# The sample tile inside the last prompt group of the delta rule, its state updates inside the output projection, and three handovers of a hybrid decoder step rearranged

## The reference

```python
def gated_delta_rule(q, k, v, g, beta, s0):          # 4 heads, keys and values 128 wide
    ...                                              # per chunk: kb, lower triangle, triangular solve -> u, w
    def step(state, inp):
        qd, kd, uc, wc, att, cd = inp
        v_new = uc - wc @ state
        out = qd @ state + att @ v_new
        state = state * cd + kd.T @ v_new
        return state, out
    s_fin, outs = lax.scan(step, s0, xs)

o, s_fin = gated_delta_rule(dq, dk, dv, g, beta, s0)   # s0 = 0 for the prompt, a given state for each sample
o = rms_norm(o, delta_norm_w) * silu(bz)
h = x + concatenate([a_out, o]) @ w_out                # output projection, 1024 x 1024
hn = rms_norm(h, norm_ffn_w)
qh = hn @ w_pq                                         # queries, 1024 x 2048
sub = einsum(qh, sub_keys)                             # scores on 2 x 128 keys, top 16 of each half, top 16 of the pairs
y = h + sum(gate * gelu(u_e . hn) * v_e)               # over the chosen experts of 16384
```

## Time and profile before

| | us |
|---|---|
| median of 3 runs | 2228.98 (2225.56 to 2231.54) |
| profiled execution | 2227.2 |
| its span, first to last instruction | 2225.4 |
| PE busy | 2014.9 (91%) |
| DVE busy | 1540.5 (69%) |
| POOL busy | 1158.6 (52%) |
| ACT busy | 771.4 (35%) |

### The profile page before, as it was taken

How to read it: one execution, slowest core, us unless ns; L and a number is a source line. 1 busy time by engine, 2 the same in 40 slices (tenths; PEclk the granted TensorE clock), 3 DMA queues, 4 the chain that set the end, 5 groups by cost and what they waited for, 6 DMA issues and landing times.

```text
span 2225.4 us, 34386 instructions
## 1 busy us (share of the span) xinstructions
PE 2014.9 (91%) x12706; PEld 1898.6 (85%) x12706; DVE 1540.5 (69%) x2782; ACT 771.4 (35%) x1228; POOL 1158.6 (52%) x632
## 2 busy tenths in 40 slices
PE   5999899787768997999898999999899999999998
PEld 5989855576658896988888998999799999999998
DVE  2377555434251105689985999964489999999996
ACT  3224144323212323444344444433323333333332
POOL 2235100123032232567576444458788888888884
PEclk9999799998759898999999999999999999999999
DMA  5664365343422354577678687789888989899894
GB/s 185 221 239 163 137 191 175 110 184 150 161 98 85 131 233 158 167 238 231 212 241 264 239 304 253 303 323 384 303 311 318 311 310 328 308 317 313 308 324 135
DMA packets 176595, 520.94 MB, mean 234 GB/s; under 512 B 15152, under 2 KB 86064, under 8 KB 170704
## 3 DMA queue, kind: packets, MB, share of 16 engines
q1 hardware_dynamic: 136560, 290.94, 37.5%
q0 software_dynamic: 36864, 134.23, 17.9%
q10 hardware_dynamic: 3056, 94.24, 10.8%
HBM read 456.81 MB, written 128.49 MB: 263 GB/s over the span
## 4 chain that ended last, share of the span: by engine, by line
PE 45%; DVE 35%; issue 7%; POOL 5%; ACT 4%; DMA 4%; SPq 0%; ACTq 0%; DVEq 0%; PEldq 0%; POOLq 0%
DVE acc_g L1883 10%; DVE act_l L1867 10%; PE bank L2241 8%; PE bank L2242 7%; PE bank L2243 7%; POOL u_lo L1706 3%; DVE one L1561 3%; PE twin L2241 2%; PE twin L2243 2%; PE twin L2242 2%; DMA rows_g<-eu_rows,idx_g 2%; DVE rows_g L1731 2%; PE bank L1337 2%; DVE one L1558 1%; ACT u_hi L1686 1%
## 5 line engine op out<-in xcount | busy, mean ns | idle before, releaser
L1706 POOL TENSOR_TENSOR u_lo<-u_raw,u_hi 128x1024 fp32r<-128x1024 f32 x128 | 315.7, 2466 | 296.5 <-ACT u_hi L1686 295.7
L2241 PE MATMUL bank<-hn_hi,u_hi 128*128 128x416 f32 x1024 | 374.9, 366 | 37.0 <-POOL u_lo L1706 34.3
L1911 POOL TENSOR_TENSOR v_lo<-v_raw,v_hi 128x1024 fp32r<-128x1024 f32 x128 | 335.6, 2623 | 68.8 <-ACT v_hi L1836 67.4
L2242 PE MATMUL bank<-hn_lo,u_hi 128*128 128x416 f32 x1024 | 363.9, 355 | 0.0
L2243 PE MATMUL bank<-hn_hi,u_lo 128*128 128x416 f32 x1024 | 362.4, 354 | 0.0
L1883 DVE SCALAR_TENSOR_TENSOR acc_g<-rows_g,coef,acc_g 128x1024 f32<-128x1024 f32 x127 | 292.8, 2305 | 17.0 <-DMA rows_g<-ev,idx_g 16.7
L2242 PE MATMUL bank<-a_lo,v_hi 128*128 128x416 f32 x768 | 269.2, 350 | 0.0
L2241 PE MATMUL bank<-a_hi,v_hi 128*128 128x416 f32 x768 | 269.1, 350 | 0.0
L2243 PE MATMUL bank<-a_hi,v_lo 128*128 128x416 f32 x768 | 269.0, 350 | 0.0
L2241 PEld LDWEIGHTS bank<-hn_hi,u_hi 128*128 128x128 f32 x1024 | 196.3, 192 | 52.7 <-POOL u_lo L1706 47.9
L1867 DVE TENSOR_TENSOR act_l<-act_l,gin 128x416 f32<-128x416 f32 x128 | 229.6, 1794 | 0.1
(11 more groups left out here) (414 smaller groups left out, 4466.5 us busy)
## 6 DMA issues: line engine op xcount, KB each, us to landing
u_raw<-eu SPq DMA_DIRECT2D x128, 512.0 KB, 5.0
v_raw<-ev SPq DMA_DIRECT2D x128, 512.0 KB, 4.6
k_s<-kc ACTq DMA_DIRECT2D x29, 1104.0 KB
v_s<-vc ACTq DMA_DIRECT2D x29, 1104.0 KB
acts_dram<-act_c SPq DMA_DIRECT2D x128, 208.0 KB, 4.2
gates_dram<-gst ACTq DMA_DIRECT2D x8, 3328.0 KB, 12.4
gin<-gates_dram SPq DMA_DIRECT2D x32, 832.0 KB, 8.6
act_l<-acts_dram SPq DMA_DIRECT2D x64, 416.0 KB, 5.8
```

The costliest lines, as they stand in the source:

```text
L1706: nc.gpsimd.tensor_tensor(out=u_lo[s][:], in0=u_raw[2 * (x % 2) + s][:], in1=u_hi[s][:].bitcast(F32), op=ALU.subtract).then_inc(dn["ulo"], 1)
L1911: nc.gpsimd.tensor_tensor(out=v_lo[f % 4][:], in0=v_raw[f % 4][:], in1=v_hi[f % 4][:].bitcast(F32), op=ALU.subtract).then_inc(dn["vlo"], 1)
L2241: nc.tensor.matmul(out, ah, bh, start=first and i == 0, stop=False)
L2242: nc.tensor.matmul(out, ah, bl, start=False, stop=False)
```

## The change

1. *Groups.* `GROUPS` becomes `[(0, 1), (2, 3, 4)]`. Tile 4 gets buffers and PSUM banks of its own (`SLOT`, `Y_BANK`, `XI_BANK`, `XT_BANK`), goes through front, level and u, w behind tile 3, and its steps 0 to 3 stand between the parts of the recurrence of tiles 2 and 3.
2. *State updates.* Spread, product and addition move into the output projection: two heads after block 14, two after block 15. The store of the states moves on SyncE behind the last output weight's load, with the norm's weight ahead of it; the load of that weight now waits for the state products, the store for the additions.
3. *First weight.* ACT splits weight 14 inside the recurrence, into a place of its own (`first_hi`, `first_lo`); POOL's half of it comes ahead of the scaling of the states. ACT splits weight 15 ahead of `cat_hi`.
4. *Norm by tiles.* In block 17 each tile is added, squared, scaled and turned as soon as its product is there; the query products start with the two that need tiles 0 to 2 alone (`QUERY_ORDER`), and tile 4 is turned between them.
5. *Start of the stream.* The keys are loaded together with `X`. ACT copies `x_held` after its loop of the first tile `t = 0`; DVE waits for it at `t == 1`.

```diff
-        GROUPS = [(0, 1), (2, 3), (4,)]
+        GROUPS = [(0, 1), (2, 3, 4)]
+        SLOT = [0, 1, 0, 1, 2]
...
         def pe_delta(pe):
...
+                for n in group:
+                    if n == NT - 1:
+                        continue
...
+                        last.then_inc(dl["ws"], 1)
+                        if n >= 2:
+                            pe_delta_sample(pe, 2 * (n - 2))
...
+                    last.then_inc(dl["os"], 1)
+                    if n >= 2:
+                        pe_delta_sample(pe, 2 * (n - 2) + 1)
...
+        def pe_sample_state(pe, h):
+            w, s = NB * NL, SLOT[NT - 1]
+            pe.wait_ge(dl["vm"], h + 1)
+            if h >= 2:
+                pe.wait_ge(dl["su"], h - 1)
+            for b2 in range(2):
+                last = nc.tensor.matmul(quad(STATE_BANKS[h % 2] + b2), kd[s][0:w, h, :], vm[h % 2][0:w, 4 * b2:4 * b2 + 4, :],
+                                        start=True, stop=True)
+            last.then_inc(dl["st"], 1)
...
         def dve_delta(dve, chain):
...
+                for n in group[0:2]:
+                    output_var(n)
+                for n in group[0:2]:
+                    output_norm(n)
+                if NT - 1 in group:
+                    output_var(NT - 1)
+                    dve.wait_ge(dl["s_act"], 2)
+                    spread_values(0)
+                    output_norm(NT - 1)
+                    spread_values(1)
...
         def sp_ffn(sp):
...
                         x = x_p[t * P:(t + 1) * P, :] if t < NT - 1 else x_s
                         sp.dma_start(X[0:TILES[t][1], t, :], x).then_inc(x_in[t], 16)
+                    sp.dma_start(skt_s[:], skt).then_inc(consts_in, 16)
+                if k == NW1 + 3:
+
+                    sp.wait_ge(dl["st"], BH)
                     sp.dma_start(nmix_b[:], nffn.partition_broadcast(P)).then_inc(consts_in, 16)
+                    sp.wait_ge(dl["su"], BH)
+                    sp.wait_ge(kv_out, 16 * (NKV + 1))
+                    sp.dma_start(s_s.rearrange("b h k v -> k (b h) v"), ss0[:]).then_inc(kv_out, 16)
             sp.wait_ge(w_used, NW3)
-            sp.dma_start(skt_s[:], skt).then_inc(consts_in, 16)
+            sp.wait_ge(kv_out, 16 * (NKV + 2))
...
         def pe_ffn(pe, product):
...
+                    if k == NW2 - 1 and t >= 2:
+                        turn_normed(t - 2)
+                if k < NW1 + 2:
+                    for h in range(2):
+                        pe_sample_state(pe, 2 * (k - NW1) + h)
...
         def act_ffn(act, chain):
-            split_weights(act, NW1)
             act.wait_ge(dl["cat"], NT)
             act.wait_ge(kv_out, 16 * (NKV + 1))
+            split_weights(act, NW1 + 1)
             for i in range(CAT_PARTS):
...
             for t, (t0, w) in enumerate(TILES):
                 act.wait_ge(ff["h_used"], (NW_OUT - 1) * NT + t + 1)
...
+                if t >= 2:
+                    normed_hi(t - 2)
+                act.wait_ge(var_ready, 1 + t + 1)
+                nc.scalar.activation(stat[0:w, 3, t:t + 1], stat[0:w, 3, t:t + 1], ACT.Sqrt).then_inc(rstd_ready, 1)
...
+                if t == 0:
+                    few_wait(act, "x_in", 32)
+                    for b in range(2):
+                        nc.scalar.activation(x_held[0:NG, 512 * b:512 * (b + 1)], xrep[0:NG, 512 * b:512 * (b + 1)], ACT.Copy)\
+                            .then_inc(sx["held"], 1)
...
         def dve_ffn(dve, chain):
...
+            for k in range(NW_OUT - 1):
+                for t in range(NT):
+                    add_heads(k, t)
+                if k < 2:
+                    for h in (2 * k, 2 * k + 1):
+                        add_state(dve, chain, h)
+                    if k == 0:
+                        spread_values(2)
+                        spread_values(3)
+            dve.wait_ge(consts_in, 16 * (NCONST + 2))
+            for t in range(NT):
+                add_heads(NW_OUT - 1, t)
+                if t >= 2:
+                    normed_lo(t - 2)
+                scale_tokens(t)
+            normed_lo(NT - 2)
+            normed_lo(NT - 1)
```

More of the change, by code:

```diff
@@ L1011, in act_delta @@
[L1011 to L1017 removed]
+                        nc.scalar.activation(yv[SLOT[n]][:], quad(1), ACT.Copy).then_inc(dl["o"], 1)
@@ new lines, in dve_delta @@
+                for n in group:
+                    if n == NT - 1:
+                        continue
+                    s = SLOT[n]
+                    if n:
+                        dve.wait_ge(dl["ws"], n)
+                        tt(out=ml[s][:], in0=uu[s][:], in1=quad(0), op=ALU.subtract).then_inc(dl["vn"], 1)
+                    if n >= 2:
+                        sample_values_new(dve, n - 2)
+                    dve.wait_ge(dl["os"], n + 1)
+                    if n:
+                        for h in range(BH):
+                            chain.mark(nc.vector.scalar_tensor_tensor(out=s_cur[:, h, :], in0=s_cur[:, h, :], scalar=eg[s][:, h, P - 1:P],
+                                                                      in1=quad(2)[:, h, :], op0=ALU.mult, op1=ALU.add))
```

452 lines of the change are left out of this document (231 added, 221 removed).

## The result

The changed kernel takes 2207.5 us (median, 2202.2 to 2207.8) against 2230.3 for the kernel before (2225.6 to 2234.1): ratio 0.9893, interval 0.9868 to 0.9918. In a later set of runs it took 2205.5 against 2228.9, ratio 0.9897 (0.9878 to 0.9916). So it is faster by some 23 us, where 34 were forecast: 12.5 us above the forecast, within the range.

The account below looks back on a forecast made before the run. No single engine bound it; handovers at three seams did. Gains of 24.6 - 1.1 + 4.5 + 6.0 = 34.0 off the profiled 2227.2 gave 2193.2, or 2195.0 us as median; range 2176 to 2212.

Parts of the forecast that it names:

- rival A: Delta rule: the samples' state product falls to half clock at once, POOL costs 10 us; about 2210 us, chance 0.18.
- Rival B: Delta rule: samples' state product at 6.2 us, no loss to POOL, half the preparation hidden; about 2182 us, chance 0.17.
- Seam 1: End of the delta rule to the first output product: last piece of cat 24.6 us earlier.
- preparation: Sample tile's front, level, u and w, moved ahead of the recurrence: 10.3 us on the path, TensorE's busy time.
- step 0: Sample tile's product of the states, between recurrence parts: taken at 8.5 us, 7.8 after 0.7 comes back (6.2 to 13.1).
- the norm with POOL: VectorE's norm of tiles 2 to 4 before cat: 12.1 us, plus 6 lost beside GpSimd (0 to 13.9).
- the forecast's +1.1: Last piece of cat to last output block: -4.5 for X, -1.8 clock dip, +7.4 state products; 1.1 us later.
- Rival D: Output and query projections: pauses for state products hold TensorE at 1.2 GHz, +78 us; about 2273 us, chance 0.03.
- Rival E: Norm before the query projection: query weight lands late behind the store, whole 4.5 us lost; 2199.5 us, chance 0.08.
- Seam 3: Start of the expert stream, 838 to 863 us: ScalarE's 6.4 us standstill goes; 6.0 us earlier (0 to 10).
- the table's 3.55: Before the expert stream: TensorE's 3.55 us wait for the key table, swallowed by ScalarE's wait for the first expert tile.
- Rival C: Stretch after 925 us: VectorE or rows fetched for it bound, 6 us given back; about 2201 us, chance 0.10.

Follow-up runs that it names:

- experiment 6: Changed kernel with ScalarE's split of the first output weight moved ahead of tile 2's output, so GpSimd's work runs earlier; ratio 0.9870 to the kernel before.
- the second execution: The changed kernel, unaltered, run and traced once more beside the kernel before: 2205.5 us against 2228.9, ratio 0.9897.
- experiment 1: Changed kernel with the sample tile back in a group of its own behind tiles 2 and 3; ratio 0.9910 to the kernel before.
- experiment 3: Changed kernel with the norm before the query projection done for all five tiles at once again; ratio 0.9911 to the kernel before.
- experiment 8: Changed kernel with ScalarE copying the held rows of x ahead of the routing loop again; ratio 0.9919 to the kernel before.
- experiment 4: Changed kernel with the sub-keys loaded behind the last query weight again; ratio 0.9898 to the kernel before.

## Why the prediction was right or wrong

**Sign and size.** Faster by 1%, as forecast with 0.94; the time fell between the forecast and rival A, nearer to A. A's clock is what happened, in a milder form: full clock for 1.2 us, then half, and tile 2's output 2.4 longer (A said 3). A's heavy toll to POOL (10) did not happen. Rival B, whose POOL was done ahead of the norm, is what experiment 6 had to build first.

**Seam 1: 24.6 forecast, 17.3 measured (15.3 in the second execution). This is where it was wrong.** The last piece of cat was to stand at 612 to 627; it stood at 632.9, which is 626.8 less the 6 us by which this trace starts late. Term by term, forecast and then measured (by experiment 1, and POOL's part by experiment 6): preparation 10.3, 13.6; step 0 7.8, 11.6; tile 2's output 0, 2.4; step 2 1.0, 0.15 (it hides behind DVE's subtraction); the norm with POOL 18.1, 16.7, of which POOL's part 6, 5.3. The first three terms came out 9.5 longer than forecast, the other two 2.2 shorter; that makes the 7.3 that are missing. The step that failed most is the choice of 8.5 for step 0 between 6.9 and 13.8 "nearer the low one, since the stretch it enters is at 1.00". Here the stretch's clock when the product entered said nothing of what it was granted (0.99 for 1.2 us, then 0.50 for 11.3); the row that showed this very product busy at 0.50 was the nearer one. From the same choice it follows that what stands behind would be slow too, and that term stood in rival A but at nothing in the forecast. The second is the preparation: PE's busy time alone was taken, with the other engines as covered; the cost lay between PE alone (10.3) and the sum of PE and ACT (18.3). That the three wait for one another in turn is read from their busy times and was not tested.

**From C to the first query product.** The last block began 0.9 later behind C than before (61.4 against 60.5), near the forecast's +1.1, with the pairs of state products at 3.7, as said. The 14.8 that this was halved from is all that PE was busy with in a stretch which the earlier trace rows leaves out, a little more than the state products:

```profile
624.00:644.00 20.00, 14.84 (x22) 5.55 (x20) 13.26 (x17) 2.23 (x4) 1.58 (x1) 0.50 0.17 49
```

The other two terms, X and the dip of the clock, were not measured one by one. Rival D did not come: from 648 to 709, with both pairs of state products, the granted clock was 1.00. The norm gained 4.9 (25.9 against 30.8) for 4.5, and 2.0 to 3.8 is left of it at the end of the queries (experiment 3). Rival E did not come: ACT split the first query weight at 694.2, and what released it was PE, not a load.

**Seam 3: 6.0 forecast, 7.0 measured at R.** The standstill for the held rows was the right mechanism (experiment 8), but "the table's 3.55 is swallowed by the load of u" was wrong at R: with the sub-keys early, ACT's first split of u stands 4.7 behind Qn, not 13.0 as before or 17.7 as in experiment 4, and the edit alone is worth 5 there. That the sum came out right was luck: two gains of 5 overlap to 7. Rival C is half right: DVE starts its first selection 15.6 nearer to Qn than before (4.9 against 20.5), and 11.8 of that goes into a longer wait for ACT, 20.4 for 8.7. Behind R the two executions of the changed kernel lose 1.8 and gain 1.9, so a return of 6, as rival C had it, is not seen; one of 2 could not be told.

**The profiled run's own offset.** The forecast took all before 495 us as equal. Single executions differ by some 6 us there, with the clock as one part of it (0.69 against 0.82 from 250 to 300). It does not decide here, but without it the first trace reads as a gain of 19.6.

## What to carry to other kernels

When a narrow product is moved into a dense stretch, price it at the clock that its own rows show, and price what stands behind it too. Dealing out a lump of it between wide products helped here (7.4 for 12.6), though the clock still fell behind some of the lots. Work of another engine that meets a chain of short operations is better started ahead of that chain (5.3 here). When work is moved off a path, look for a wait that the receiving engine has anyway: the same state products cost 3.3 us between two blocks and nothing ahead of the first. An experiment that undoes one part should be read in the trace for what else it moves, as POOL's work in experiment 1. And where two edits remove waits that lie side by side, undo each alone: their gains do not add.

## What was not expected of the hardware

- TensorE's granted clock fell to 0.50 in the middle of gapless work (busy 11.30 of 11.30 us at 0.50), and which of the products it meets differs from one execution to the next: the same step 0 took 12.60 and 13.66.
- On VectorE a scalar operation on 128x4 elements took 1.04 us beside a GpSimd operation and 0.17 alone.
- A load of the sub-keys at the head of the queue delayed the first use by 12.1 us, more than the 3.55 that the kernel before showed for the same load; why it took longer there was not tried.
